# A float32 layer pair on one core: the high and low half of the activations meet the high weights in one product of 512 columns

## Reference

```python
zin = rmsnorm(x, gain) @ w_in          # layer 1: q, k, v, g_attn, u, g_pool, m_attn, m_pool
y_attn = (stick_breaking_attention(q, k, v) * silu(g_attn)) @ w_attn_up
y_pool = (mixed * pool_scale * silu(g_pool)) @ w_pool_up
x = x + (sigmoid(m_attn) * y_attn + sigmoid(m_pool) * y_pool) @ w_out
...
proj = h @ w_in                        # layer 2: rq, rk, rv, rg, gqkv, ga, gb, gz, gate_a, gate_b
merged = sigmoid(gate_a) * yr + sigmoid(gate_b) * yg
x = x + merged @ w_out
x = x + cross_attention(h, mem_n, w_q, w_kv, w_o)
x = x + jnp.square(jax.nn.relu(h @ w_ff1)) @ w_ff2
```

## Time and profile before

| | |
|---|---|
| time, median of 3 runs | 3107.37 us (3105.9 to 3107.63) |
| profiled execution: its time, its span | 3102.98 us, 3101.2 us |
| PE busy | 3024.7 us (98%) |
| DVE busy | 1774.6 us (57%) |
| ACT busy | 1451.8 us (47%) |
| HBM read | 499.01 MB, 162 GB/s over the span |

### The profile page before, as it was taken

How to read it: one execution, slowest core, us unless ns; L and a number is a source line. 1 busy time by engine, 2 the same in 40 slices (tenths; PEclk the granted TensorE clock), 3 DMA queues, 4 the chain that set the end, 5 groups by cost and what they waited for, 6 DMA issues and landing times.

```text
span 3101.2 us, 56203 instructions
## 1 busy us (share of the span) xinstructions
PE 3024.7 (98%) x24600; PEld 2980.7 (96%) x24600; DVE 1774.6 (57%) x2324; ACT 1451.8 (47%) x1749; POOL 29.6 (1%) x60
## 2 busy tenths in 40 slices
PE   8999999999999999999999999999999999999997
PEld 8999999999999999999999989999999999999997
DVE  7543455576655566767766764455455555555455
ACT  5334544365333355666665654344335333444343
POOL 0001100000000000000000000000000000000000
PEclk9999999999999999999999999999999999999999
DMA  6443345454444433333333334544344445454543
GB/s 261 175 176 123 136 181 186 190 226 164 164 178 175 163 141 135 123 123 123 122 117 130 123 137 176 178 176 160 126 169 162 181 183 190 178 190 178 190 178 122
DMA packets 71141, 504.75 MB, mean 163 GB/s; under 512 B 7888, under 2 KB 8016, under 8 KB 11120
## 3 DMA queue, kind: packets, MB, share of 16 engines
q1 hardware_dynamic: 70416, 497.16, 43.6%
q0 software_dynamic: 336, 3.80, 0.3%
q10 hardware_dynamic: 144, 0.18, 0.0%
HBM read 499.01 MB, written 2.10 MB: 162 GB/s over the span
## 4 chain that ended last, share of the span: by engine, by line
PE 73%; issue 18%; DVE 4%; ACT 3%; POOL 1%; DMA 0%; SPq 0%; ACTq 0%; DVEq 0%
PE bank L1084 72%; PE bank L1087 1%; DVE wlo L1738 1%; ACT whi L1437 1%; POOL sp L2360 1%; DVE Alo L1744 0%; DMA hs<-in_hsT 0%; DVE Alo L1738 0%; ACT L1629 0%; ACT L1622 0%; ACT L1454 0%; DVE cacc L1744 0%; DVE gz L1738 0%; DVE dM L1738 0%; DVE mblk L1744 0%
## 5 line engine op out<-in xcount | busy, mean ns | idle before, releaser
L1084 PE MATMUL bank<-Ahi,whi 128*128 128x256 f32 (+2 forms) x5648 | 1623.8, 287 | 29.0 <-DVE wlo L1738 13.0
L1084 PE MATMUL bank<-Alo,whi 128*128 128x256 f32 (+2 forms) x5648 | 1601.3, 284 | 0.0
L1084 PE MATMUL bank<-Ahi,wlo 128*128 128x256 f32 (+2 forms) x5648 | 1600.3, 283 | 0.0
L1437 ACT ACTIVATE whi<-raw 128x1024 fp32r<-128x1024 f32 x930 | 929.8, 1048 | 821.4 <-PE bank L1084 808.9
L1738 DVE TENSOR_TENSOR wlo<-raw,whi 128x1024 fp32r<-128x1024 f32 x930 | 1103.0, 1217 | 254.9 <-ACT whi L1437 254.6
L1084 PEld LDWEIGHTS bank<-Ahi,whi 128*128 128x128 f32 (+1 forms) x5648 | 1081.9, 192 | 38.8 <-issue 17.9
L1084 PEld LDWEIGHTS bank<-Alo,whi 128*128 128x128 f32 (+1 forms) x5648 | 1081.6, 192 | 2.8 <-issue 1.3
L1084 PEld LDWEIGHTS bank<-Ahi,wlo 128*128 128x128 f32 (+1 forms) x5648 | 1080.9, 191 | 0.2
L1084 PE MATMUL bank<-Bhi,whi 128*128 128x256 f32 x1280 | 363.0, 284 | 0.0
L1084 PE MATMUL bank<-Blo,whi 128*128 128x256 f32 x1280 | 362.7, 283 | 0.0
L1084 PE MATMUL bank<-Bhi,wlo 128*128 128x256 f32 x1280 | 362.7, 283 | 0.0
(11 more groups left out here) (320 smaller groups left out, 1926.1 us busy)
## 6 DMA issues: line engine op xcount, KB each, us to landing
raw<-in_wall SPq DMA_DIRECT2D x463, 1024.0 KB, 4.8
X<-in_xT SPq DMA_DIRECT2D x1, 2048.0 KB, 10.8
Mm<-in_memT POOLq DMA_DIRECT2D x1, 2048.0 KB, 14.1
mblk<-in_memT SPq DMA_DIRECT2D x8, 256.0 KB, 5.4
out<-Mx SPq DMA_DIRECT2D x8, 256.0 KB, 2.1
dec<-in_dec POOLq DMA_DIRECT2D x1, 1536.0 KB, 7.8
hs<-in_hsT SPq DMA_DIRECT2D x2, 544.0 KB, 7.5
raw<-in_wall SPq DMA_DIRECT2D x2, 512.0 KB, 5.8
```

What stands on the lines that cost most here:

```text
L1084: return q.matmul(out, lhsT, rhs, start=start, stop=stop, skip_group_check=True)
L1437: q.activation(whi[j % SPL][:, c], raw[j % RAW][:, c], ACT.Copy).then_inc(S("w_hi"), 1)
```

## The change

In pairs of kind T (and G) the product of the high weights with the high activations and that with the low activations become one matmul: `AA` holds `Ahi` and `Alo` side by side (`BB` does for B), so that the moving operand is `AA[:, :, o:o+256]`, 2 x 256 = 512 columns, and its output a whole PSUM bank. The low weights by high activations stay a matmul of 256 columns, which adds to the first half of that bank. The two halves of a bank are the two sums, and they are added on eviction: a `reduce_sum` over a view of the two banks of a pair (1024 columns in, 512 out, `summed`), and after it the multiplication that the eviction was before, now in place in SBUF; for the residual two additions in place of one. An accumulator is now a pair of banks (`double`), of which there are 2; the side work has 4 banks throughout. `rv` and `mv` are made in pairs of 512 output columns with 512 moving weight columns, 4 units each of 4 tiles. `mk` is evicted by DVE, not ACT. Kind W keeps its products of 272 columns.

```diff
-        for i in range(2):
-            add("rv", 2 * h + i, "w_in_2", 2048 + 512 * h + 256 * i)
+        add("rv", h, "w_in_2", 2048 + 512 * h, nu=4, kt=4, nc=512)
...
-    main, side, tmp = Ring([0, 1, 2, 3]), Ring([4, 5, 6, 7]), Ring([0, 1, 2, 3])
+    main, side, tmp = Ring([0, 1]), Ring([2, 3, 4, 5]), Ring([0, 1, 2, 3])
...
+        s = 0 if stage in ("u", "k", "v", "gab", "res", "rv", "mk", "mv") else up("sum")
+        return add(stage, idx, b=b, full=full, sum=s, ev=up(by), **more)
+
+    def emptied(r):
+        return ("sum", r["sum"]) if r["sum"] else ("ev", r["ev"])
...
-    main.places.remove(3)
-    side.places.append(3)
-    side.freed[3] = main.freed[3]
...
-        pair("T", "mk", phase4, ev_act("mk"), half=True)
+        pair("T", "mk", phase4, ev_plain("mk"), half=True)
...
+    double = [nc.alloc_psum_tensor(f"double{i}", [P_, 1024], F32) for i in range(2)]
+    bank = {i: nc.alloc_psum_tensor(f"bank{i}", [P_, 512], F32) for i in range(2, 6)}
...
+                    elif kind == "N":
+                        o = out[:, m * 512:(m + 1) * 512]
+                        mm_group(o, hh[:, cs], wh[:, i, :], start=first, stop=False)
+                        mm_group(o, hh[:, cs], wl[:, i, :], start=False, stop=False)
+                        ins = mm_group(o, hl[:, cs], wh[:, i, :], start=False, stop=last)
                     else:
+                        n, c = (nc_, slice(0, nc_)) if kind == "G" else (128, cs)
+                        mm_group(out[0:n, m * 512:m * 512 + 2 * T], wh[:, i, c], both, start=first, stop=False)
+                        ins = mm_group(out[0:n, m * 512:m * 512 + T], wl[:, i, c], hh, start=False, stop=last)
...
+        def summed(out, r):
+
+            both = double[r["b"]][:, :].rearrange("p (m x t) -> p m t x", m=2, x=2)
+            q.reduce_sum(out, both, mybir.AxisListType.X).then_inc(S("sum"), 1)
+            q.wait_ge(S("sum"), r["sum"])
...
             g = f2(gz[h % 2])
-            tt(gz[h % 2][:, :, :], two(bank[r["b"][0]][:, :]), rb2, ALU.mult).then_inc(S("ev"), 1)
+            summed(gz[h % 2][:, :, :], r)
+            tt(gz[h % 2][:, :, :], gz[h % 2][:, :, :], rb2, ALU.mult).then_inc(S("ev"), 1)
...
-            tt(X2(j), bank[r["b"][0]][:, :], X2(j), ALU.add).then_inc(S("ev"), 1)
+            x, (hi, lo) = X[:, 2 * j:2 * j + 2, :], parts(r)
+            tt(x, hi, x, ALU.add).then_inc(S("res_hi"), 1)
+            own_res[0] += 1
+            q.wait_ge(S("res_hi"), own_res[0])
+            tt(x, lo, x, ALU.add).then_inc(S("ev"), 1)
```

More of the change, by code:

```diff
@@ L63, in pairs @@
         add("mk", j, "w_xkv_2", 256 * j)
-    for j in range(8):
-        add("mv", j, "w_xkv_2", 2048 + 256 * j)
+    for j in range(4):
+        add("mv", j, "w_xkv_2", 2048 + 512 * j, nu=4, kt=4, nc=512)
     for j in range(8):
@@ L217, in pair @@
         done["pair"] += 1
-        banks = [main.take() for _ in range(2 if kind == "W" else 1)]
+        bank, freed = main.take()
         last = done["unit"] + nu
-        P.pairs.append({"kind": kind, "tag": tag, "idx": idx, "nu": nu, "kt": kt, "nc": nc, "banks": banks, "ready": ready})
+        P.pairs.append({"kind": kind, "tag": tag, "idx": idx, "nu": nu, "kt": kt, "nc": nc, "bank": bank, "freed": freed, "ready": ready})
         for k in range(nu):
@@ L235, in pair @@
             if k == nu - 1:
-                name, value = evac(tag, idx, [b for b, _ in banks], last)
-                for b, _ in banks:
-                    main.free(b, name, value)
+                name, value = evac(tag, idx, bank, last)
+                main.free(bank, name, value)
             slot()
@@ L305, in f @@
         def f(tag, j, bs, full):
-            return "ev", evac(stage, j, bs, full)["ev"]
+            return emptied(evac(stage, j, bs, full))
         return f
@@ L368, in f @@
             gate[0] = t
-            return "ev", evac(stage, j, bs, full, t=t, tf=tf, sig=up("sig"))["ev"]
+            return emptied(evac(stage, j, bs, full, t=t, tf=tf, sig=up("sig")))
         return f
@@ L395, in ev_au @@
     def ev_au(tag, j, bs, full):
-        r = evac("au", j, bs, full, t=gate[0], m=up("merged"))
-        tmp.free(gate[0], "merged", r["m"])
-        return "ev", r["ev"]
+        t2, tf2 = tmp.take()
+        r = evac("au", j, bs, full, t=gate[0], t2=t2, tf2=tf2, m=up("merged"))
+        tmp.free(gate[0], "ev", r["ev"])
+        tmp.free(t2, "merged", r["m"])
+        return emptied(r)
     phase_b2 = ("b_lo", [at["ga", k // 2]["lo"] for k in range(8)])
@@ L568, in make_plan @@
         pair("T", "rk", phase3, ev_plain("rk"))
-        for i in range(2):
-            pair("N", "rv", phase3, ev_plain("rv"))
+        pair("N", "rv", phase3, ev_plain("rv"))
         for i in range(2):
@@ L742, in f @@
         def f(tag, j, bs, full):
-            return "eva", evac(stage, j, bs, full, by="eva")["ev"]
+            return "eva", add(stage, j, b=bs, full=full, ev=up("eva", 2))["ev"]
         return f
     for j in range(8):
-        pair("T", "mk", phase4, ev_act("mk"), half=True)
+        pair("T", "mk", phase4, ev_plain("mk"), half=True)
     drain()
-    for j in range(8):
+    for j in range(4):
         pair("N", "mv", phase4, ev_act("mv"))
@@ L885, in program @@
     wlo = [ar.get([P_, UNIT], F32R, f"wlo{i}") for i in range(SPL)]
-    Ahi_off = ar.off
-    Ahi = ar.get([P_, NT * L], F32R, "Ahi")
-    Alo_off = ar.off
-    Alo = ar.get([P_, NT * L], F32R, "Alo")
+    A_off = ar.off
+    AA = ar.get([P_, 2, NT * L], F32R, "AA")
+    Ahi, Alo = AA[:, 0, :], AA[:, 1, :]
     X = ar.get([P_, NT, T], F32, "X")
@@ L1103, in mm @@
             pr = P.pairs[pi]
-            kind, banks = pr["kind"], [b for b, _ in pr["banks"]]
+            kind, out = pr["kind"], double[pr["bank"]]
             if k == 0 and half == 0:
-                for _, f in pr["banks"]:
-                    free(f)
+                free(pr["freed"])
             q.wait_ge(S("w_lo"), 2 * j + half + 1)
@@ L1898, in s_au @@
         def s_au(j, r):
+            free(r["tf2"])
+            full(r)
+            x = tmps[r["t2"]][:, :]
+            summed(two(x), r)
             q.wait_ge(S("sig"), at["ma", j]["sig"])
-            full(r)
-            x = tmps[r["t"]][:, :]
-            tt(x, bank[r["b"][0]][:, :], x, ALU.mult).then_inc(S("ev"), 1)
+            tt(x, x, tmps[r["t"]][:, :], ALU.mult).then_inc(S("ev"), 1)
             q.wait_ge(S("ev"), r["ev"])
@@ L2122, in s_conv @@
             full(r)
[L2123 removed]
+            x = cst[:, :, 3:T + 3]
+            summed(x, r)
+            tt(x, x, rb2, ALU.mult).then_inc(S("ev"), 1)
         def conv_taps(key, m, value):
@@ L2288, in s_memlo, with s_mk @@
             split_low(lambda j: mblk[j][:, :])(j, at["memn", j])
+        def s_mk(j, r):
+            full(r)
+            q.wait_ge(S("a_lo"), at["memn", j]["lo"])
+            both = double[r["b"]][:, :].rearrange("p (m x t) -> p m t x", m=2, x=2)
+            q.reduce_sum(two(kpc[j][:, :]), both, mybir.AxisListType.X).then_inc(S("ev"), 1)
         def s_xq(j, r):
```

146 lines of the change are left out of this document (78 added, 68 removed).

## The result

The changed kernel takes 3079.3 us (median of 4 runs, 3074.15 to 3083.33), the kernel before beside it 3106.69 us: a ratio of 0.9911, 95% interval 0.9894 to 0.9928. The forecast was 3040 us. The direction was right and the time lies in the range of 3010 to 3088 us, but of 67 us expected 27 came.

The account below looks back on a forecast made before the run. PE, busy for 98% of the span, was taken as the bound. Its stream would shorten by 95 us and longer evictions cost 28 us, 67 us less than 3107.4: 3040 us, with 3010 to 3088 us holding 8 in 10.

Parts of the forecast that it names:

- Columns at 2.4 GHz and the same excess: PE stream: a fused 512-column matmul takes 0.2269 us, the excess beyond its columns being that of a 256-column one.
- kind N: rv and mv on PE: 512 groups at 0.3606 us become 256 at 0.6807 us, 10.4 us less.
- Kind T outside layer 1: PE stream: 5632 groups of three matmuls go from 0.3606 to 0.3471 us each, 76.0 us less.
- a rival at 0.09: PE stream: the excess goes with the columns, 512 take up to 0.2404 us, 3139 us in all; chance 0.09.
- a slow reduction: DVE evictions: the reduction takes 2.3 to 2.4 us, 3085 us in all; chance 0.17.
- The longer evictions: Places where PE waits for DVE or ACT: later evictions there cost 28 us in all, clock included.
- gz: Gated delta stage, each head: the line through ACT's sigmoid to Mn moves, 1.3 us x 8 heads = 10.4 us.
- Where f2 follows f1: FFN: the first f2 pair waits for Blo of the last f1 pair, 0.2 us x 8 = 1.6 us.
- The clock: Gated delta heads: longer waits drop PE to the lower clock level in three of seven, 5 us, bounds 0 and 12.
- The edits at nothing: Two double accumulators, one side-work bank less, third temporary in au, rv and mv, mk off ACT: no cost.
- the waits don't come: Gated delta: DVE is earlier at gz and the clock stays, only some 8 us lost, 3020 us; chance 0.13.
- PE waits for an accumulator: Gated delta: PE waits behind DVE's queue, 1 us more in each of 40 pairs, 3080 us; chance 0.06.

Follow-up runs that it names:

- gz_three: Changed kernel, with three products of 256 columns and evictions of 512 elements for gz and gtb only (16 pairs); 3067.14 us, ratio 0.9873.
- fused_single: Changed kernel with the fused product, but each eviction reads only the first half of each bank, without the sums; 3052.23 us.
- three_sum: Changed kernel without the fused product: kind T again has three products of 256 columns, sums on eviction stay; 3125.33 us.
- after_again: The changed kernel once more, unchanged, for a second profile; 3077.35 us.
- three_single: Changed kernel with three products of 256 columns and evictions of 512 elements; double accumulators, side-work banks, rv, mv and mk stay as changed; 3100.15 us.
- before_weights_shifted: Kernel before the change, with high and low split weights 16 columns (64 bytes) further on in SBUF; 3038.25 us, ratio 0.978.
- three_weights_shifted: Changed kernel with three products of 256 columns, evictions of 512 elements and the split weights 16 columns further on; 3021.62 us, ratio 0.9729.
- three_shifted_again: Three products, evictions of 512 elements, changed rings and split weights 16 columns on, once more in more executions; 3026.77 us, ratio 0.9766.

## Why the prediction was right and wrong

- **The step that failed** is "Columns at 2.4 GHz and the same excess make 0.1067 + 0.1202 = 0.2269 us, which fits, and I take it", with what was built on it: 0.3471 us for every k-tile and half outside the first layer, and 0.0096 us less for those in it. The excess beyond the columns is no constant of the instruction. A 512-column product among its own kind does take 0.2267 us, and kind N, where only such products follow each other, gave 10.1 us of 10.4. Between products of 256 columns it takes 0.230 to 0.241 us: on average 0.230 us in wo2, at the one speed of the stream, and 0.236 us in xo, at the other, and the 256 columns behind it take 0.117 us in both. Together that is 0.3467 us, as forecast, or 0.3533 us; the mean of the FFN is 0.3516 us. Kind T outside layer 1 gained about 51 us, not 76.0 (48 in the four groups of stages from f1 to xo in the table, 3.3 in pu and au), and the first layer's A tiles about 0, not 8.6. The prediction had the sign in hand, an excess of 0.0096 us in one stretch and 0.0135 us in the other, "no constant of the instruction", and used it for a rival at 0.09 only; the likeliest case kept it constant. (By the starts of the products the first layer's k-tile and half was 0.3506 to 0.3513 us before, not 0.3489 us: the windows also count matmuls that still run when they begin.)
- **The time in the range** is no support for the sum: the range reached up to 3088 us for a slow reduction, at 3085 us, and the reduction took 1.224 us as forecast.
- **The price of a removed matmul.** The Trainium skill ("TensorE: Matmul & The Clock Gate", section "Back-to-back issue gap") gives N/2.4 + 2.5 ns at the full clock, from which the prediction worked out 2.5 ns for each removed matmul. The runs don't bear that out either: 61 us for 7296 of them are 8.4 ns each. With the weights 16 columns on, 256 columns take 0.1133 us, 6.7 ns above the columns; no run here shows 2.5 ns.
- **The longer evictions** were right in sum, 28 us forecast, 25.2 and 27.1 measured, and right at gz, 1.40 for 1.3 us a head; what hangs on gz and gtb alone is worth 12 us (gz_three; 10.4 + 0.8 and some of the clock forecast). Where f2 follows f1, two groups of each block's first f2 pair take 0.467 to 0.548 and 0.452 to 0.465 us, not 0.350 (in fused_single there is no such place): 2.0 us for eight blocks, forecast 1.6. Missed were DVE's queue in wo, 4 us there, and 3 us at gab. That the sum still fits is in part luck: the 3 us counted for retention didn't come (387.1 us from rq to gab in fused_single, 387.2 in the changed kernel).
- **The clock** can count for more than the sum had: granted over the span it is 0.987 in three_sum and in the changed kernel (0.989 in after_again), 0.991 and 0.993 in three_single and fused_single, 0.992 before. 0.004 to 0.006 of 3090 us are 12 to 18 us at most, for 5 counted; what of it PE really lost wasn't measured apart, and it is part of the 25 to 27 us.
- **The edits at nothing** cost nothing that is clear of the noise, 3 us by the medians: the stream of kind N is 10.1 us shorter, and rings, kind N and `mk` together brought 7 us (5 to 10 by the interval of three_single). From mk's first product to mv's it took 117.4 us in three_single and 115.1 us before.
- **The rivals.** That the excess goes wholly with the columns fell with kind N; the slow reduction with 1.224 us; that the waits don't come with the waits at gz; that PE waits for an accumulator with its list. None of them was what happened: a stream with two speeds.

What physically holds a product back by where its two operands start stays open; shown are the dependence and its size.

## What to carry to other kernels

Don't price a fused or widened product by a constant beyond its columns: run the very group alone, at several phases and with the operands at several starts within 256 bytes, before evictions are made longer for it. What a longer eviction costs can be counted from the trace at the places where PE already waits, and only there; leaving those pairs (here 16) in the old form gets half of it back. And 64 bytes between two arrays were worth 2.2 to 2.5% here (before_weights_shifted against the kernel before, three_weights_shifted and three_shifted_again against three_single), more than twice the 0.9% of the change; but the same 64 bytes made the changed kernel 17 us slower.

## What the runs showed of the hardware

- Three 256-column fp32r products take from 0.3400 to 0.3667 us with the same instructions, by the starts of stationary and moving operand and by phase (in the kernels 0.3400, 0.3533, 0.3567 or 0.3600 us). With both at the same place of 256 bytes it was 0.3600 us at each phase tried, and outside waits in every such stretch of the kernel before.
- A speed is kept for thousands of products, 700 us of FFN in before_weights_shifted, and changes at a wait of PE, or where products of another form come between (kind N in retention).
- A product of 512 columns starts its follower after 0.2267 us among its own kind, after 0.230 to 0.241 us between products of 256.
- With 64 stationary columns in place of 128 the next 256-column product starts after 0.1133 us, not 0.1200; with 32 it isn't less.
